# Router of a hybrid backbone step: the last tile's rows in two halves around the mask, its logits chain ahead of its squares, first lists within the ranking, down loads ahead of gate rows

## The reference

```python
h = rmsnorm(x, norm2) * (1 + scale2) + shift2
p_grp = softmax(t @ w_grp)                 # 4 groups
p_g, g_idx = top_k(p_grp, 1)
sel = e_logits[:, g_idx]                   # 8 experts of the chosen group
top_w, top_i = top_k(softmax(sel), 2)      # two experts of 32 for each token
act = silu(t @ w_gate[e]) * (t @ w_up[e]) * combine
out = sum over e of act @ w_down[e]        # w_up, w_gate 1024x256, w_down 256x1024
x = x + gate2 * out;  y = rmsnorm(x, final_norm)
```

## Time and profile before

| | before |
|---|---|
| median of 3 runs | 943.6 us (942.42 to 944.73) |
| profiled execution, its own time | 942.75 us |
| its span | 940.5 us |
| PE busy | 877.8 us (93%) |
| DVE busy | 416.1 us (44%) |
| ACT busy | 277.3 us (29%) |
| POOL busy | 111.2 us (12%) |
| data moved | 198.83 MB, mean 211 GB/s |

### The profile page before, as it was taken

The page is one execution under the profiler, slowest core; times in us unless marked ns, Lnnn a source line. Parts: engine busy times, 40 slices in busy tenths (PEclk is TensorE's granted clock), DMA queues, the critical chain, the costliest instruction groups (busy, mean ns, idle before and its releaser), DMA issues. The chain is left out here.

```text
span 940.5 us, 15004 instructions
## 1 busy us (share of the span) xinstructions
PE 877.8 (93%) x6016; PEld 695.0 (74%) x6016; DVE 416.1 (44%) x892; ACT 277.3 (29%) x522; POOL 111.2 (12%) x123
## 2 busy tenths in 40 slices
PE   3798988989999999999999999995899999999997
PEld 3587666777899999999999998884555555555552
DVE  1358345445534343351521266538534344343433
ACT  5336654445620311212121232333111111111122
POOL 0000000000000000000000021021232333323330
PEclk9899999999999999999999999997799999999999
DMA  9945443622213212212223222779999999999948
GB/s 330 352 175 187 153 188 110 192 66 68 66 53 90 76 59 89 88 46 89 68 71 130 68 90 73 240 255 352 383 412 416 415 414 416 413 416 414 415 184 334
DMA packets 73679, 198.83 MB, mean 211 GB/s; under 512 B 11384, under 2 KB 43112, under 8 KB 61080
## 3 DMA queue, kind: packets, MB, share of 16 engines
q1 hardware_dynamic: 65800, 181.71, 51.9%
q0 software_dynamic: 7824, 16.36, 4.6%
HBM read 189.30 MB, written 18.17 MB: 221 GB/s over the span
## 5 line engine op out<-in xcount | busy, mean ns | idle before, releaser
L810 PE MATMUL pair<-w_ug,xgT 128*64 128x256 f32 x1184 | 138.3, 387 | 1.2 <-ACT xgT L947 1.2
L1904 DVE TENSOR_TENSOR lo<-raw,hi 128x2048 fp32r<-128x2048 f32 (+3 forms) x32 | 69.4, 2168 | 114.0 <-ACT hi L1721 113.2
L1721 ACT CAST hi<-raw 128x2048 fp32r<-128x2048 f32 (+3 forms) x31 | 53.8, 1734 | 218.1 <-PE pair L1345 202.1
L1343 PE MATMUL pair<-hT,hi 128*128 128x320 f32 x512 | 116.7, 309 | 0.0
L1345 PE MATMUL pair<-hT,lo 128*128 128x320 f32 x512 | 116.7, 309 | 0.0
L1341 PE MATMUL pair<-hT,hi 128*128 128x320 f32 x512 | 116.6, 309 | 0.0
L810 PEld LDWEIGHTS pair<-w_ug,xgT 128*64 128x64 f32 x1184 | 84.8, 139 | 42.0 <-issue 4.5
L1341 PEld LDWEIGHTS pair<-hT,hi 128*128 128x128 f32 x512 | 85.6, 188 | 0.2 <-issue 0.2
L1345 PEld LDWEIGHTS pair<-hT,lo 128*128 128x128 f32 x512 | 85.7, 188 | 0.0
L1343 PEld LDWEIGHTS pair<-hT,hi 128*128 128x128 f32 x512 | 85.5, 188 | 0.0
L829 PE MATMUL pair<-w_dn,actT 128*64 128x512 f32 x296 | 71.7, 605 | 1.3 <-issue 1.3
(11 more groups left out here) (350 smaller groups left out, 1467.4 us busy)
## 6 DMA issues: line engine op xcount, KB each, us to landing
w_ug<-in_w_up SPq DMA_DIRECT2D x32, 1024.0 KB, 21.6
w_ug<-in_w_gate SPq DMA_DIRECT2D x32, 1024.0 KB, 24.3
w_dn<-in_w_down SPq DMA_DIRECT2D x32, 1024.0 KB, 21.2
raw<-in_w_in SPq DMA_DIRECT2D x20, 1024.0 KB, 5.3
ada_a<-in_w_ada SPq DMA_DIRECT2D x14, 1024.0 KB, 11.3
raw<-in_w_ada SPq DMA_DIRECT2D x10, 1024.0 KB, 6.3
ya<-expert_rows SPq DMA_DIRECT2D x5, 1024.0 KB, 9.1
raw<-in_w_conv_out SPq DMA_DIRECT2D x4, 1024.0 KB, 5.0
```

The source lines that it names most:

```text
L810: x = pe.matmul(bank[2 + d % 2][g * SL:(g + 1) * SL, 0:DE], xgT[d % 2][:, k, h * SL:(h + 1) * SL], w_ug[r][:, g, h, k, :], start=(n == 0), ...
L1343: pe.matmul(o, st[0], m[1], start=False, stop=False)
L1721: act.copy(hi[n % 2][:, 0:size], raw[n % 4][:, 0:size]).then_inc(hi_done, 1)
L1904: dve.tensor_sub(lo[n % 2][:, 0:size], raw[n % 4][:, 0:size], hi[n % 2][:, 0:size].bitcast(F32)).then_inc(lo_done, 1)
```

## The change

Five things are moved; no operation is added or taken away.

1. The last tile's logits chain goes ahead of its squares on ACT. The four `lg_scale` come before `x1T_out(1, 4)`, and that before the squares. For this, PE's `logits_turn(3)` comes ahead of the last `x1_turn`, the last turn waits for all scalings too, and tiles 3 and 4 get other PSUM places. DVE's addition for the first four tiles comes before the last tile's reciprocal.
2. The last tile's row operation is split: the first half of the row before the last `lg_rows`, the second inside `dve_moe`, behind the mask and the two differences; s_h2g rises only then.
3. The first four lists (with their wait for FIRST_PS) come before the ranking.
4. The copy of the experts' numbers (with its wait for NUMBERS) comes before `spill`.
5. On SP, the down loads of experts 1 and 2 come before the gate2 rows.

```diff
--- before.py
+++ after.py
@@ -526,15 +526,15 @@
 
         sp.wait_ge(s_mixe, 2 * NT)
         load_down(0, 0)
+        sp.wait_ge(s_lg, NT)
+        for p in range(1, PRE - 1):
+            load_down(p, p)
         sp.wait_ge(s_h2g, NT)
         for st in range(2):
             for h in range(2):
                 sp.dma_start(gate2[h * SL:(h + 1) * SL, st, :].rearrange("p (g c) -> p g c", g=2),
                              MODW[3].rearrange("(g r) c -> g r c", g=4)[2 * h:2 * h + 2, st].partition_broadcast(SL)
                              ).then_inc(s_g2, 16)
-        sp.wait_ge(s_lg, NT)
-        for p in range(1, PRE - 1):
-            load_down(p, p)
 
         def ranked(p):
             return sp.value_load(expert_i[0:1, ORDER[p]:ORDER[p] + 1], min_val=0, max_val=NE - 1)
@@ -704,12 +704,12 @@
         x.then_inc(s_lg, 1)
 
     def lgT_of(i):
-        b, n = ((6, 0), (6, 1), (7, 0), (7, 1), (0, 0))[i]
+        b, n = ((6, 0), (6, 1), (7, 0), (0, 0), (1, 0))[i]
         return bank[b][:, n * 36:n * 36 + 36]
 
     def logits_turn(pe, i):
 
-        pe.wait_ge(s_lge, i + 1)
+        pe.wait_ge(s_lge, i + 1 if i < NTS else NTS + NT)
         pe.matmul(lgT_of(i), lg36[:, i * P:(i + 1) * P], cst[0:100, K_SEL:K_SEL + NG + NE], start=True, stop=True
                   ).then_inc(s_lgT, 1)
 
@@ -921,17 +921,16 @@
         for i in range(NT):
             if i == NT - 1:
                 lg_out(act, i - 1)
+                for i_ in range(NTS):
+                    lg_scale(act, i_)
+                x1T_out(act, 1, i)
             squares(act, link, 1, i)
+            root(act, i)
             if i < NT - 1:
-                root(act, i)
-            x1T_out(act, 1, i)
+                x1T_out(act, 1, i)
             if 1 <= i < NT - 1:
                 lg_out(act, i - 1)
-            if i == NT - 1:
-                root(act, i)
         lg_out(act, NT - 1)
-        for i in range(NTS):
-            lg_scale(act, i)
 
         act.wait_ge(s_exp_in, 1)
         act.activation(r_ge[:, :, :], r_gs[:, :, :], ACT.Exp).then_inc(s_exp, 1)
@@ -974,7 +973,7 @@
             act.activation(stat[:, R3 + 8 + i:R3 + 9 + i], stat[:, R3 + i:R3 + i + 1], ACT.Sqrt,
                            scale=1.0 / D, bias=stat[:, 95:96]).then_inc(s_rms3, 1)
 
-    def dve_moe(dve, link):
+    def dve_moe(dve, link, row_half):
         def wide(ap, n):
             return ap.unsqueeze(2).to_broadcast([P, NT, n])
 
@@ -998,6 +997,7 @@
         dve.tensor_add(mask[:, :, :], hot[:, 0], hot[:, 1]).then_inc(s_route, 1)
         dve.tensor_sub(r_gs[:, :, :], gl, wide(r5[0][:, :], NG)).then_inc(s_exp_in, 1)
         dve.tensor_sub(r5[3][:, :], r5[2][:, :], r5[1][:, :]).then_inc(s_exp_in, 1)
+        row_half(NTS, 1).then_inc(s_h2g, 1)
 
         iota = cst[:, K_IOTA:K_IOTA + NE]
         place, beyond, tile, slot, past = (r[:, :, :] for r in r10)
@@ -1032,22 +1032,22 @@
         link(dve.scalar_tensor_tensor(out=key, in0=raw_x, scalar=-ROUND, in1=cst[0:NE, K_KEY:K_KEY + NE + 1],
                                       op0=ALU.add, op1=ALU.add))
         dve.tensor_scalar(more, raw_x[:, NE:NE + 1], -ROUND, None, ALU.add)
+        dve.wait_ge(s_route_ps, FIRST_PS)
+        link(dve.tensor_scalar(r_l[:, 0:PRE], bank[7][:, 128:128 + PRE], cst[:, K_HALF:K_HALF + 1], None, ALU.add))
+        dve.tensor_add(lists[:, 0, 0:PRE], bank[7][:, 128 + PRE:128 + 2 * PRE], r_l[:, 0:PRE]).then_inc(s_rdy, 1)
         link(dve.tensor_scalar(over_[:, 0:NE], key[:, 0:NE], key[:, NE:NE + 1], None, ALU.is_gt))
         link(dve.tensor_reduce(rank, over_[:, 0:NE], AXX, ALU.add))
         dve.tensor_scalar(rows_b[:, 0:NE], iota[0:NE, :], rank, None, ALU.is_equal).then_inc(s_route, 1)
-        dve.wait_ge(s_route_ps, FIRST_PS)
-        link(dve.tensor_scalar(r_l[:, 0:PRE], bank[7][:, 128:128 + PRE], cst[:, K_HALF:K_HALF + 1], None, ALU.add))
-        dve.tensor_add(lists[:, 0, 0:PRE], bank[7][:, 128 + PRE:128 + 2 * PRE], r_l[:, 0:PRE]).then_inc(s_rdy, 1)
         dve.tensor_scalar(q4, rank, float(PRE), None, ALU.is_equal)
         link(dve.tensor_scalar(room, rank, float(PRE), None, ALU.is_ge))
         link(dve.scalar_tensor_tensor(out=room, in0=rank, scalar=float(PRE + 4), in1=room, op0=ALU.is_lt, op1=ALU.mult))
         link(dve.tensor_add(room, room, q4))
+        dve.wait_ge(s_route_ps, NUMBERS)
+        dve.tensor_copy(expert_i[0:1, 0:NE], bank[6][0:1, 64:64 + NE]).then_inc(s_extra, 1)
         link(dve.tensor_tensor(spill, more, room, ALU.is_gt))
         link(dve.tensor_mul(left, more, spill))
         link(dve.tensor_copy(lx_b[:, :], left))
         dve.sem_inc(s_route)
-        dve.wait_ge(s_route_ps, NUMBERS)
-        dve.tensor_copy(expert_i[0:1, 0:NE], bank[6][0:1, 64:64 + NE]).then_inc(s_extra, 1)
         link(dve.scalar_tensor_tensor(out=given, in0=rank, scalar=float(EXT - PRE), in1=q4, op0=ALU.add,
                                       op1=ALU.subtract))
         dve.tensor_copy(tab_b[:, 0:1], rank)
@@ -1697,8 +1697,8 @@
         mix(1, 1, 4, range(2, 4))
         logits(pe, 3)
         logits_turn(pe, 2)
+        logits_turn(pe, 3)
         x1_turn(pe, 1, 4)
-        logits_turn(pe, 3)
         logits(pe, 4)
         logits_turn(pe, 4)
         pe_moe(pe)
@@ -2206,16 +2206,21 @@
                 dve.wait_ge(h2_w[0], 16)
             link(dve.tensor_mul(in_fours(h2_rows[i % 4][:, :]), by_fours(x1[:, i, :]), by_fours(gain2[:, stream[i], :])))
 
-        def row_shift(i):
+        def row_root(i):
             dve.wait_ge(s_rms2, i + 1)
             link(dve.reciprocal(stat[:, 64 + i:65 + i], stat[:, R2 + 8 + i:R2 + 9 + i]))
+
+        def row_half(i, h):
+            rows = in_fours(h2_rows[i % 4][:, :])[:, h]
+            return dve.scalar_tensor_tensor(out=rows, in0=rows, scalar=stat[:, 64 + i:65 + i],
+                                            in1=by_fours(shift2[:, stream[i], :])[:, h], op0=ALU.mult, op1=ALU.add)
+
+        def row_shift(i):
+            row_root(i)
             if i == 0:
                 dve.wait_ge(s_sh2, 32)
-            for h in range(2):
-                rows = in_fours(h2_rows[i % 4][:, :])[:, h]
-                x = dve.scalar_tensor_tensor(out=rows, in0=rows, scalar=stat[:, 64 + i:65 + i],
-                                             in1=by_fours(shift2[:, stream[i], :])[:, h], op0=ALU.mult, op1=ALU.add)
-            x.then_inc(s_h2g, 1)
+            row_half(i, 0)
+            row_half(i, 1).then_inc(s_h2g, 1)
 
         dve.wait_ge(s_g1, 32)
         for i in range(NT):
@@ -2253,12 +2258,13 @@
         row_shift(3)
         add_y(1, NT - 1)
         row_gain(4)
-        row_shift(4)
-        dve.wait_ge(s_lge, NT + NTS)
+        dve.wait_ge(s_lge, 2 * NTS)
         link(dve.tensor_add(lg[:, 0:NTS, :], lg[:, 0:NTS, :], shift_bc[:, 0:1, :].to_broadcast([P, NTS, NG + NE])))
+        row_root(4)
+        row_half(4, 0)
         dve.wait_ge(s_lgT, NT)
         lg_rows(NTS)
-        dve_moe(dve, link)
+        dve_moe(dve, link, row_half)
 
     es.close()
```

## The result

The changed kernel takes 949.03 us in the median of 15 runs (947.07 to 952.09), the kernel before, run beside it, 945.10 (942.20 to 948.34, 15 runs). The ratio is 1.0046 with a 95% interval of 1.0034 to 1.0059, so it is slower by 4.3 us (3.2 to 5.6). The forecast was 944.5, +0.9, with a range to 947.0: outside. (The forecast was counted from a median of 943.6 in three runs; 15 runs gave 945.10 for the same kernel, so 1.5 of the 4.5 us between 944.5 and 949.03 lies in the starting point. The change itself costs 4.3 where 0.9 was forecast.) The profiled execution took 948.24 (span 945.8), 5.3 us more in its span than the one before.

A forecast was written before the change was run, and what follows sets the result against it. The first expert tile's start was taken to bound the kernel. The -0.43 and small terms lay on chains not ending last; the late write's +0.9 on the 943.6 median gave 944.5 us, range 942.3 to 947.0.

The forecast's parts named there:

- What bounds: Experts' stage: its tiles run back to back on PE, so the kernel's end follows the first tile's start one to one.
- The last tile's logits: Router, last lg row on DVE: runs at 647.72 instead of 648.15, a gain of 0.43 us.
- The second half behind the mask: DVE ahead of first_val: 0.71 us of row work, partly covered by idle time, costs +0.25 us.
- The lists: DVE's first list operations, run ahead of the ranking: end at 657.70 instead of 658.30, 0.60 us earlier in all.
- PE's queue at L764: PE's routing work up to the first gathered rows' transposes: shifts by +0.11 us, putting L798 at 663.04 by that queue.
- The last rows' write: POOL's h_rows write, issued at 654.78, lands 4.4 us later and holds the first gather, which starts 0.88 us late.
- The gather itself stays at 3.6.: First gather of expert rows: its time from issue to landing stays 3.6 us, so L798 starts at about 663.8.
- Rival 2: Last tile's row write takes 6.3 us or more beside gate rows: gather +2.8, 946.4 us, at 8.7 948.8; chance 0.14.
- Rival 1: Last tile's row write lands in under 4 us, so PE's queue ends last: +0.1, 943.7 us; chance 0.22.
- the early clock: PE's clock rises before the first expert tile: 2.47 us gained and 0.9 lost, 942.0 us; chance 0.05.
- The down loads moved ahead ... come to nothing: SP's loads: swapping the order of down loads and gate rows costs nothing, bounded by +-0.1 us.
- The Trainium skill's fit: Write from POOL's queue: 2.0 us plus bytes at 436 GB/s, 3.2 us for 512 KB; trusted for an idle DMA only.

The follow-up runs named there:

- numbers back: The changed kernel with the copy of the experts' numbers put back behind the spill; ratio to the kernel before 1.0051 (1.0026 to 1.0075).

## Why the prediction was wrong

- What bounds: right. The end follows the first tile, and the experts' stage passes the delay on in full but for the clock.
- The last tile's logits: -0.48 at the last lg row for -0.43. The second half behind the mask: 0.22 given back for 0.25. The lists: -0.68 for -0.60 (-0.44 in the means over all profiles). PE's queue at L764: +0.02 for +0.11. Right.
- The last rows' write: issued at +10.85, for which the sum had +10.86. It landed 5.0 later where I took 4.4; the gather started 1.49 late for 0.88. The mechanism was right and the size 0.6 short.
- **The step that failed: "The gather itself stays at 3.6."** It took 7.3, which is 3.7 of the 5.2 us at L798 (the other 1.5 is the start). The 3.6 in the earlier trace rows was measured where SP's first load of a ranked expert came 1.4 behind it. I computed that the numbers would come some 0.5 sooner and wrote "nobody waits for them", and that the gather would start 0.88 later, and did not lay the two beside each other: 0.88 and 0.5 make 1.38, the whole lead of 1.39, and a gather that starts level with the load already takes 7.3 (numbers back). As it came, the gather started 1.49 later and the load 0.72 sooner. The later gathers, with 6.7 to 6.9 in the same profile, had the price.
- Rival 2 (a write of 6.3 or more) foresaw a loss of this size, from another cause: the write took 5.0 here, and no more than 5.2 in any kernel that issued it behind the mask. Rival 1 and the early clock did not come about; the clock did give back 0.88, which I had counted at nothing.
- "The down loads moved ahead ... come to nothing": right for the time in the medians (0.9995 for this part alone), not for the write, which takes 8.8 to 10.9 beside them where it is early, and in two profiles holds the gather.
- The Trainium skill's fit (DMA: Bandwidth & Descriptors, Anatomy of one DMA), an estimate of 3.2 us for the write, is below all landings here, 4.3 at the least where it ran beside gate rows alone. The measurements decide.

The crossing over all runs: with the gather 1.3 to 2.1 ahead of the load, L798 followed it by 3.6 to 4.3 (in the 4.34 the gather had landed after 3.4 and PE's queue held L798); with it 0.76 ahead, by 5.2; level or up to 0.98 behind, by 7.3 to 7.8. Twice a wait that keeps the load away brought it back to 3.4 and 3.6. How the engines choose between the two queues is not shown by these runs, only that q0 had no packet in the stretch and that a load kept away takes the delay with it.

## What to carry to other kernels

Where a small transfer on the critical path runs shortly ahead of a stream of large loads, its duration in the trace holds only for that order: write down by how much it is ahead, and when an edit delays it or hastens the loads, price it with the duration of its kind beside a full load. A start that slips by 1.5 us can cost 5. If it must slip, hold the loads until it has landed; here one wait brought back 4.4 us at L798 and 3.5 at the last tile's start, and the ratio fell from 1.0046 to 1.0023. Then look at the end of the kernel, whose loads are now later too: there the hold brought a new wait of 0.3.

## What else the runs showed

The first tile's products took between 5.13 and 6.62 us over the profiles, all beginning at the lower clock, so about 1.5 us of a run's time lies in when the clock rises after they start. And the last x1 came at 643.5 to 648.3 us; the first tile's row write, ahead of which all the kernels are alike, was issued at 631.43 to 636.21, so nearly all of that spread arises before the router. The last tile's row write of 512 KB took 4.3 to 5.2 us beside gate rows, 6.2 to 7.5 beside loads that had begun before it, and 8.8 to 10.9 beside three down loads in a row.
